# Corner products of 64x64 in place of block-diagonal 128x128 matrices in a chunked WKV recurrence

## The chip, the cores and the metric

One core of one Trainium2 chip runs the whole program, all in float32. The metric is the device time in microseconds of one execution. Engines are named as in the profile: PE is TensorE, PEld its weight loads, DVE is VectorE, ACT is ScalarE, POOL is GpSimd, SP issues most DMAs.

## The reference, cut to what matters

The program is a two-block network on 512 tokens with 256 context tokens. The first block mixes tokens by three methods, one of which is a recurrence over time with four heads of width 64, run in both directions:

```python
def wkv_scan(state0, r, kk, v, decay, b, k, reverse):
    def step(S, inp):
        r_t, kk_t, v_t, w_t, b_t, k_t = inp
        sa = jnp.einsum('bhij,bhj->bhi', S, kk_t)
        S = S * w_t[:, :, None, :] - sa[..., None] * b_t[:, :, None, :] + v_t[..., None] * k_t[:, :, None, :]
        return S, jnp.einsum('bhij,bhj->bhi', S, r_t)
    return lax.scan(step, state0, (r, kk, v, decay, b, k), reverse=reverse)
```

For each direction the 256 context tokens come first, then the 512 latent tokens start from the context's last state. Only latent outputs are used. Before and after the recurrence stand projections, two kinds of attention, a mixture of experts over 16384 rows, and a second block with its own attention and feed-forward layers.

## The kernel before, in words

The kernel doesn't step through tokens. It cuts time into 12 chunks of 64 tokens (0 to 3 context, 4 to 11 latent), and works each chunk in closed form: products of keys and values inside the chunk, the inverse of a 64x64 unit triangular matrix, and an update of the 64x64 state. There are eight such problems: two directions `d`, four heads. A head is `64*a` to `64*a+63` of the partitions with `a` 0 or 1, and a group `g`; the free index `s` is `2*d + g`, 0 to 3. So one PE step handles `s` = 0 to 3, each for two heads.

Before the change the two heads of an `s` stand in one 128x128 matrix as two diagonal blocks, with zeros off the diagonal; a matrix for all `s` is 128x512 and fills a PSUM bank. `Chunk.diagonal_blocks` (L1113) sets out `AB, BB, KB, VB, NT, M2`; `rwkv_zero_pool` (L1319) and L1521 zero their corners once.

`chunks` (L1748) takes chunks in pairs, and lets the two chunks of a pair take turns, step by step, on every engine; each engine runs its own in-order program and waits by semaphores. A chunk's part has three stretches.

- First products: `N`, `M1`, `M2` (L1420), masked by DVE (L1588, L1598, L1602), and the transposes `Bt`, `T0`, `Kt`, `Vt` (L1428), copied by ACT (L1552).
- The inverse: levels 1 to 4, each `X` = `NTo`' `Ta` (L1435, copied by ACT), `A` = `Tb`' `Xs` (L1435, added to `Ta` by DVE at L1613), and a transpose of `Ta` back to `Tb` (L1428, copied by DVE at L1617 or ACT). POOL masks `NTo` for the next level (L1632). Then `Y` and `inverse` close with two more products (L1621).
- The state, chunk by chunk: `RH` (L1673, L1674), its negative on DVE (L1713), `U` (L1681), copy (L1717), `sum` (L1688, L1689), add (L1721), four scalings (L1728). Latent chunks add the outputs (L1701 to L1703, L1740). The state update of a chunk needs that of the chunk before.

DVE, ACT and POOL prepare the inputs of chunk c+2 (`chunk_inputs_*`) between the levels of chunk c. PSUM banks: 0 to 2 for even chunks, 3 to 5 for odd ones, 6 and 7 for the state. After the recurrence come `first_half_pe` and the expert stage; eight loads of `w_out` wait for `state_filled` of chunk 10 (`out_weights_sp`).

Of the kernel before, what the change touches and what calls it, by code (L numbers as in the profile page):

```python
# [123 lines left out]
def constants():  # L124
# [966 lines left out]
MASKS = (("m_bk", 256), ("m_kk", 256), ("m_first", 128), ("m_last", 128), ("m_level", 256))  # L1091
# [4 lines left out]
class Chunk:  # L1096
# [3 lines left out]
    def __init__(self, A, B, ring, blocks_first, second, e1):  # L1100
        self.E1, self.KR = [B.take(2, 2, 65), e1.take(2, 2, 65)], [B.take(4, 2, 64), second.take(4, 2, 64)]
        if blocks_first:
            self.diagonal_blocks(A)
        self.at = A.at
        self.Bt, self.Kt, self.Vt, self.Ta, self.Tb, self.No, self.NTo = (A.take(4, P) for _ in range(7))
        self.M1R, self.M2R = A.take(4, 64), A.take(4, 64)
        self.E2 = second.take(2, 2, 64)
        self.Xs = A.take(4, P)
        if not blocks_first:
            self.diagonal_blocks(A)  # L1110
        self.AB = [self.AB, second.take(4, P)]
        self.ring = ring

    def diagonal_blocks(self, A):
        at = A.at
        self.AB, self.BB, self.KB, self.VB, self.NT, self.M2 = (A.take(4, P) for _ in range(6))
        self.blocks = A.t[:, at:A.at].rearrange("p (m s a n) -> p m s a n", m=6, s=4, a=2)
# [5 lines left out]
def rwkv_memory(k, rw, A):  # L1123
# [21 lines left out]
    rw.idb = k.ident[:, None, :].to_broadcast([P, 4, P])  # L1145
# [5 lines left out]
    rw.sets = [Chunk(slots, A, (0, 1, 2), False, free[0], Arena(k.SUMSQ, T)),  # L1151
               Chunk(A, A, (3, 4, 5), True, free[1], Arena(rw.Z[:, 8, :], TK))]
# [166 lines left out]
def rwkv_zero_pool(k, p):  # L1319

    S, rw = k.S, k.rw
    p.e.memset(rw.YT, 0.0).then_inc(*p.up(S.pool_scaled))
    p.wait_ge(S.ada_turned, 1)
    for j in (1, 0):
        for a in range(2):
            rows = slice(64 * a, 64 * a + 64)
            for m in range(6):
                p.in_order()
                p.e.memset(rw.sets[j].blocks[rows, m, :, 1 - a, :], 0.0).then_inc(
                    *(p.up(S.blocks_zeroed, j) if a and m == 5 else p.up(S.pool_scaled)))  # L1330
# [69 lines left out]
def by_direction(x):  # L1400

    return x.rearrange("p (d g n) -> p d g n", d=2, n=64)


def chunk_pe(k, p, c):
    S, rw = k.S, k.rw
    B, nk, x = rw.sets[c % 2], 2 if c >= 4 else 1, c // 2 % 2
    AB, KR = B.AB[x], B.KR[x]
    yield
    p.wait_ge(S.chunk_kept, (c, "inputs" if c >= 4 else "keys"))  # L1410
    p.wait_ge(S.chunk_prepared, (c, "inputs"))
    p.wait_ge(S.chunk_copied, (c, "inputs"))
    for step, (name, left, right, w) in enumerate((
            ("N", AB, lambda s: B.BB[:, s, :], P),
            ("M1", B.BB, lambda s: KR[:, s, 0:nk, :], 64 * nk),
            ("M2", B.KB, lambda s: KR[:, s, 0:nk, :], 64 * nk))):
        bank = chunk_bank(k, B, c, step)
        p.claim(chunk_place(B, c, step), S.chunk_kept, (c, name))
        for s in range(4):
            ins = p.e.matmul(bank[:, s * P:s * P + w], left[:, s, :], right(s), start=True, stop=True, skip_group_check=True)  # L1420
        ins.then_inc(*p.up(S.chunk_filled, (c, name)))
        yield

    def turned(step, name, src, signal):
        bank = chunk_bank(k, B, c, step)
        p.claim(chunk_place(B, c, step), signal, (c, name))
        for s in range(4):
            ins = p.e.transpose(bank[:, s * P:s * P + P], src[:, s, :], k.ident)  # L1428
        ins.then_inc(*p.up(S.chunk_filled, (c, name)))

    def products(step, name, left, right, signal):
        bank = chunk_bank(k, B, c, step)
        p.claim(chunk_place(B, c, step), signal, (c, name))
        for s in range(4):
            ins = p.e.matmul(bank[:, s * P:s * P + P], left[:, s, :], right[:, s, :], start=True, stop=True, skip_group_check=True)  # L1435
        ins.then_inc(*p.up(S.chunk_filled, (c, name)))

    turned(3, "Bt", B.BB, S.chunk_copied)
    yield
    p.wait_ge(S.chunk_kept, (c, "Ta"))  # L1440
    turned(4, "T0", B.Ta, S.chunk_copied)
    yield
    turned(5, "Kt", B.KB, S.chunk_copied)
    yield
    p.wait_ge(S.chunk_prepared, (c, "values"))
    turned(6, "Vt", B.VB, S.chunk_copied)
    yield
    for l in range(1, 5):
        p.wait_ge(S.chunk_prepared, (c, "NTo", l))
        products(4 + 3 * l, f"X{l}", B.NTo, B.Ta, S.chunk_copied)  # L1450
        yield
        p.wait_ge(S.chunk_copied, (c, f"X{l}"))
        p.wait_ge(S.chunk_copied if l % 2 else S.chunk_kept, (c, f"T{l - 1}"))
# [4 lines left out]
        yield  # L1458
    p.wait_ge(S.chunk_copied, (c, "T4"))
    products(19, "Y", B.No, B.Tb, S.chunk_copied)  # L1460
    yield
    p.wait_ge(S.chunk_copied, (c, "Y"))
    products(20, "inverse", B.Ta, B.Xs, S.chunk_kept)
    yield


def chunk_inputs_act(k, p, c):
# [13 lines left out]
    if c >= 4:  # L1481
        p.wait_ge(S.state_filled, (c - 4, "last"))
    p.wait_ge(S.chunk_kept, (c, "keys"))
    for a, h in enumerate(HEAD):
        p.e.activation(B.AB[x][h, :, h], B.KR[x][h, :, 0, :], ACT.Copy).then_inc(
            *(p.up(S.chunk_copied, (c, "inputs")) if a else p.up(S.scalar_step)))
    yield


def chunk_inputs_dve(k, p, c):  # L1490
# [23 lines left out]
def chunk_inputs_pool(k, p, c):  # L1514
    S, rw = k.S, k.rw
    B = rw.sets[c % 2]
    if c in (2, 3):
        p.wait_ge(S.bonus_product, 1)
        for a, h in enumerate(HEAD):
            p.in_order()  # L1520
            p.e.memset(B.AB[1].rearrange("p s (a n) -> p s a n", a=2)[h, :, 1 - a, :], 0.0).then_inc(*p.up(S.pool_scaled))  # L1521
# [3 lines left out]
    for h in HEAD:  # L1525
        p.in_order()
        p.e.tensor_tensor(B.KB[h, :, h].rearrange("p (d g) n -> p d g n", d=2), windows(rw.Kd, c, h), B.E2[h], ALU.mult).then_inc(
            *(p.up(S.chunk_prepared, (c, "inputs")) if h.start else p.up(S.pool_scaled)))
    yield
    if c >= 2:  # L1530
        p.wait_ge(S.chunk_filled, (c - 2, "Vt"))
    for d in range(2):
        for h in HEAD:
            p.in_order()
            p.e.tensor_copy(B.VB[h, SL[d], h], window(rw.V, c, d)[h]).then_inc(
                *(p.up(S.chunk_prepared, (c, "values")) if d and h.start else p.up(S.pool_scaled)))
# [3 lines left out]
def chunk_act(k, p, c):  # L1540
# [15 lines left out]
    for step, name, dst in ((3, "Bt", B.Bt), (4, "T0", B.Tb), (5, "Kt", B.Kt), (6, "Vt", B.Vt)):  # L1556
        copied(step, name, dst)
        yield
    for l in range(1, 5):
        copied(4 + 3 * l, f"X{l}", B.Xs)  # L1560
        yield
        if l in (1, 4):
            next(coming, None)
        yield
        if l % 2 == 0:
            copied(6 + 3 * l, f"T{l}", B.Tb)
        elif l == 1:
            next(coming, None)
        yield
    copied(19, "Y", B.Xs)  # L1570
    yield
    yield


def chunk_dve(k, p, c):
# [2641 lines left out]
```

## Time and profile before

| | |
|---|---|
| time, median of 3 runs | 3856.1 us (3851.97 to 3873.37) |
| the profiled execution's own time | 3852.21 us |
| its span | 3850.4 us |
| mean granted TensorE clock | 0.919 of 2.4 GHz |
| busy: PE, PEld, DVE, ACT, POOL | 85%, 63%, 55%, 20%, 36% |
| recurrence | 468.4 to 809.0 us of the span |

The profile gives one row for each of the two passes that a float32 product is run in, so a step of four products shows 8 matmul records and 8 weight loads; a transpose shows one. A form such as `128*128 128x64` reads: stationary operand 128 rows by 128 columns, moving operand 128 partitions by 64 columns. Records of the same kind that follow closely are merged in a timeline row: the second number is the time from the first's start to the last's end.

### The profile page before, as it was taken

What the parts mean: (1) busy time and instruction counts of PE and PEld (TensorE: products, weight loads), DVE (VectorE), ACT (ScalarE), POOL (GpSimd) and SP (SyncE); (2) the same over time, 40 slices, a digit from 0 to 9 for tenths busy, and PEclk for the clock granted to TensorE, in tenths of its full rate; (3) what the DMA queues carried; (4) which work ended last, traced back from release to release, by engine and by line L of the source; (5) the groups of instructions that cost most, each with busy time, mean ns of one, the idle gap of its engine ahead of it and who ended that gap; (6) DMA issues with size and microseconds to landing.
All of it is one profiled execution on the core that took longest, in us unless ns stands there. A gap on an engine that the chain in (4) does not pass through costs nothing. (4 is left out here: it accounts for less than half of the span.)

```text
span 3850.4 us, 39434 instructions
## 1 busy us (share of the span) xinstructions
PE 3280.3 (85%) x14438; PEld 2437.0 (63%) x14438; DVE 2121.7 (55%) x4234; ACT 764.9 (20%) x1791; POOL 1384.7 (36%) x1218
## 2 busy tenths in 40 slices
PE   8889888887677978647788888889897999999999
PEld 3566478775233535326567776667785778887787
DVE  2341345548889888867777668776653320133201
ACT  2231233222111111112420012320013210122100
POOL 0930022105677777754355546545500000000000
PEclk9998899998888989878689999889998999999999
DMA  6412100017999999987689999889941134431342
GB/s 206 129 66 82 31 1 1 13 44 275 363 368 373 373 374 384 393 308 276 208 288 376 394 377 371 302 282 392 394 145 34 60 125 150 147 99 61 126 152 100
DMA packets 424598, 831.77 MB, mean 216 GB/s; under 512 B 40467, under 2 KB 266830, under 8 KB 424398
## 3 DMA queue, kind: packets, MB, share of 16 engines
q0 software_dynamic: 147456, 536.94, 37.2%
q1 hardware_dynamic: 276950, 292.31, 23.3%
q8 instruction: 116, 1.90, 0.2%
q14 instruction: 76, 0.62, 0.0%
HBM read 826.98 MB, written 2.17 MB: 215 GB/s over the span
## 5 line engine op out<-in xcount | busy, mean ns | idle before, releaser
L2828 PE MATMUL banks<-arena 128*128 128x256 f32 (+1 forms) x4992 | 1142.4, 388 | 74.4 <-DMA arena<-in_l_w_up 30.4
L2828 PEld LDWEIGHTS banks<-arena 128*128 128x128 f32 (+1 forms) x4992 | 965.4, 195 | 236.8 <-issue 36.2
L2375 POOL DMA_INDIRECT arena<-in_peer_u,arena x512 | 577.6, 1128 | 456.4 <-DVE arena L2505 175.4
L2375 POOL DMA_INDIRECT arena<-in_peer_v,arena x512 | 590.5, 1153 | 400.5 <-DVE arena L2491 242.3
L2505 DVE CUSTOM_DVE_ANT_0 arena<-arena 128x1024 f32<-128x1024 f32 x512 | 628.1, 1227 | 104.4 <-DMA arena<-in_peer_u,arena 86.4
L2447 PE MATMUL banks<-arena 128*128 128x512 f32 x768 | 415.5, 685 | 188.5 <-ACT arena L2466 123.6
L2491 DVE SCALAR_TENSOR_TENSOR arena<-arena 128x1024 f32<-128x1024 f32 x316 | 406.3, 1286 | 29.4 <-DMA arena<-in_peer_v,arena 18.7
L2447 PEld LDWEIGHTS banks<-arena 128*128 128x128 f32 x768 | 159.7, 218 | 401.1 <-issue 246.4
L3737 PE MATMUL banks<-arena 128*128 128x256 f32 x1408 | 310.5, 378 | 0.0
L3786 DVE TENSOR_TENSOR arena<-banks,arena 128x512 f32<-128x512 f32 x44 | 30.5, 692 | 504.9 <-PE banks L2828 504.6
L3737 PEld LDWEIGHTS banks<-arena 128*128 128x128 f32 x1408 | 265.7, 189 | 38.3
L3758 ACT ACTIVATE arena<-banks 128x512 f32<-128x512 f32 x44 | 26.3, 597 | 684.7 <-PE banks L2828 679.7
L3279 DVE CUSTOM_DVE_ANT_0 arena<-banks,arena 128x256 f32<-128x256 f32 (+3 forms) x128 | 59.8, 467 | 138.6 <-PE banks L3161 131.4
L2140 PE MATMUL banks<-arena 128*128 128x512 f32 (+1 forms) x320 | 126.0, 542 | 9.4 <-DMA arena<-in_peer_q_w 5.9
L1632 POOL TENSOR_TENSOR arena<-arena 128x512 f32<-128x512 f32 x48 | 52.4, 1091 | 223.5 <-DVE arena L1598 119.1
L552 PE MATMUL banks<-arena 128*128 128x512 f32 (+1 forms) x336 | 132.1, 553 | 0.0
L812 PE MATMUL banks<-arena 128*128 128x512 f32 (+1 forms) x320 | 120.2, 525 | 5.7 <-ACT arena L455 3.6
L1552 ACT ACTIVATE arena<-banks 128x512 f32<-128x512 f32 x132 | 77.0, 597 | 223.9 <-PE banks L1428 173.2
L3231 ACT ACTIVATE arena<-arena 128x256 f32<-128x256 f32 (+3 forms) x128 | 69.3, 542 | 254.2 <-DVE arena L3279 185.0
L3202 PE MATMUL banks<-arena 128*128 128x64 f32 (+1 forms) x720 | 117.0, 296 | 1.5 <-ACT arena L3249 1.5
L3202 PEld LDWEIGHTS banks<-arena 128*128 128x128 f32 x720 | 111.8, 224 | 4.5 <-issue 2.6
L1435 PE MATMUL banks<-arena 128*128 128x128 f32 x960 | 114.5, 278 | 0.0
(341 smaller groups left out, 3883.7 us busy)
## 6 DMA issues: line engine op xcount, KB each, us to landing
arena<-in_l_w_gate SPq DMA_DIRECT2D x44, 1024.0 KB, 5.5
arena<-in_l_w_up SPq DMA_DIRECT2D x44, 1024.0 KB, 6.1
arena<-in_l_w_down SPq DMA_DIRECT2D x44, 1024.0 KB, 5.1
arena<-in_ada_w SPq DMA_DIRECT2D x24, 1024.0 KB, 7.6
arena<-in_l_w_qkv SPq DMA_DIRECT2D x24, 1024.0 KB, 6.4
arena<-in_w_in SPq DMA_DIRECT2D x33, 512.0 KB, 4.1
arena<-in_l_w_out SPq DMA_DIRECT2D x16, 1024.0 KB, 5.4
arena<-in_peer_q_w SPq DMA_DIRECT2D x10, 1024.0 KB, 12.4
```

The source lines that it names most:

```text
L552: ins = p.e.matmul(k.bank[b][0:m, 0:n], k.W[slot][:, c, 0:m], rhs(c), start=c == 0, stop=c == c_n - 1, skip_group_check=True)
L812: ins = p.e.matmul(k.bank[b][0:m, 0:n], k.W[slot][:, c, 0:m], rhs(c), start=c == 0, stop=c == c_n - 1, skip_group_check=True)
L1435: ins = p.e.matmul(bank[:, s * P:s * P + P], left[:, s, :], right[:, s, :], start=True, stop=True, skip_group_check=True)
L1552: p.e.activation(flat(dst), chunk_bank(k, B, c, step), ACT.Copy).then_inc(*p.up(S.chunk_copied, (c, name)))
L2140: ins = p.e.matmul(k.bank[4][:, cols], ws[:, c, P * j:P * j + P], k.HT[:, c, cols], start=c == 0, stop=c == DC - 1, skip_group_check=True)
L2375: p.e.indirect_dma_start(e.ring[slot], None, tables[table], bass.IndirectOffsetOnAxis(ap=e.IDX[h][:, t, j:j + 1], axis=0)).then_inc(*p.up( ...
L2447: ins = p.e.matmul(k.bank[b], e.diag[x % 4], e.ring[slot][:, half * T:half * T + T], start=h == 0 and j == 0, stop=h == HEADS - 1 and j == ...
L2491: p.e.scalar_tensor_tensor(out=e.ACC[t], in0=e.ring[slot], scalar=factor, in1=e.ACC[t], op0=ALU.mult, op1=ALU.add).then_inc(*p.up(S.rows_a ...
L2505: p.e.tensor_tensor_reduce(out=e.prod, in0=e.ring[slot], in1=e.H2[:, t, :], scale=1.0, scalar=0.0, op0=ALU.mult, op1=ALU.add, accum_out=e. ...
L2828: ins = p.e.matmul(out, left(c), right(c), start=c == 0, stop=c == c_n - 1, skip_group_check=True)
L3202: ins = p.e.matmul(k.bank[5][:, 0:x.w], a.PT[u % 2][:, j * P:j * P + P], values, start=j == 0, stop=j == len(x.values) - 1, skip_group_che ...
L3737: ins = p.e.matmul(k.bank[4 + o // 2][:, o % 2 * TH:o % 2 * TH + TH], w[:, r, P * o:P * o + P], a.hid[:, (i - 1) % 2, TH * r:TH * r + TH], ...
```

## The change

The two heads of an `s` now stand one above the other, 128x64 for each `s`, 128x256 for all, without zeros. Each product is of 64x64 corners: rows `HEAD[a]` as stationary and moving operand, output on partitions `HEAD[a]`. A step is eight matmuls in the order `CORNERS`, whose direction picks one of two neighbouring banks (a slot). PSUM becomes four slots of two banks, two for each chunk of a pair; the state uses slots 1 and 3 in turn. The inverse keeps both `Ta` and its transpose `Tb`: at each level `A` is added to `Ta` and `T` = `Xs`' `Tb` to `Tb`. There are five levels and no `Y`. The transposes `Bt`, `Kt`, `Vt` are products with an identity corner; `Vt` reads `rw.V` itself. `AB`, `VB`, the zeroing memsets and the copies into `AB` and `VB` go. In `state_pe`, `M2 Vt` and `Kt Vt` stand ahead of the waits. POOL also makes the first `Tb`. The loads, all other stages and the order of the stages are as before.

```diff
+STEPS = 20
+CORNERS = (0, 0), (1, 2), (0, 1), (1, 3), (1, 0), (0, 2), (1, 1), (0, 3)
+def slot_bank(slot, s):
+    return 2 * slot + s // 2
+def corner(k, slot, a, s, w=64):
+    return k.bank[slot_bank(slot, s)][HEAD[a], s % 2 * w:s % 2 * w + w]
+def slot_all(k, slot, w=64):
+    return k.PS[:, 1024 * slot:1024 * slot + 1024].rearrange("p (d x) -> p d x", d=2)[:, :, 0:2 * w].rearrange(
+        "p d (g n) -> p d g n", n=w)
+def chunk_slot(B, c, step):
+    return B.slots[(c // 2 * STEPS + step) % 2]
 def chunk_pe(k, p, c):
+    def products(step, name, left, right, signal, w=64):
+        slot = chunk_slot(B, c, step)
+        claim_slot(p, slot, signal, (c, name))
+        for a, s in CORNERS:
+            ins = p.e.matmul(corner(k, slot, a, s, w), left(a, s), right(a, s), start=True, stop=True, skip_group_check=True)
+        ins.then_inc(*p.up(S.chunk_filled, (c, name)))
...
-    turned(3, "Bt", B.BB, S.chunk_copied)
+    products(3, "Bt", of(B.BB), one, S.chunk_copied)
...
-    for l in range(1, 5):
+    for l in range(1, 6):
+        p.wait_ge(S.chunk_kept, (c, f"A{l - 1}"))
         p.wait_ge(S.chunk_prepared, (c, "NTo", l))
-        products(4 + 3 * l, f"X{l}", B.NTo, B.Ta, S.chunk_copied)
+        products(3 + 3 * l, f"X{l}", of(B.NTo), of(B.Ta), S.chunk_copied)
...
-        products(5 + 3 * l, f"A{l}", B.Tb, B.Xs, S.chunk_kept)
-        p.wait_ge(S.chunk_kept, (c, f"A{l}"))
-        turned(6 + 3 * l, f"T{l}", B.Ta, S.chunk_kept if l % 2 else S.chunk_copied)
-    products(19, "Y", B.No, B.Tb, S.chunk_copied)
-    products(20, "inverse", B.Ta, B.Xs, S.chunk_kept)
+        if l < 5:
+            products(4 + 3 * l, f"A{l}", of(B.Tb), of(B.Xs), S.chunk_kept)
+        products(5 + 3 * l if l < 5 else 19, f"T{l}", of(B.Xs), of(B.Tb), S.chunk_kept)
 def chunk_inputs_act(k, p, c):
-    for a, h in enumerate(HEAD):
-        p.e.activation(B.AB[x][h, :, h], B.KR[x][h, :, 0, :], ACT.Copy)
 def chunk_inputs_dve(k, p, c):
-    for h in HEAD:
-        p.e.tensor_tensor(B.BB[h, :, h]..., windows(rw.Bd, c, h), B.E2[h], ALU.mult)
+    p.e.tensor_tensor(by_direction(B.BB), windows(rw.Bd, c), B.E2, ALU.mult)
 def state_pe(k, p, c, between):
+    slot = state_slot(rw)          # 1 + 2 * (rw.turn % 2)
+    claim_slot(p, slot, S.state_kept, (c, "RH"))
+    p.wait_ge(S.chunk_kept, (c, "M2"))
+    p.wait_ge(S.chunk_copied, (c, "Vt"))
+    for a, s in CORNERS:
+        p.e.matmul(corner(k, slot, a, s), B.M2[HEAD[a], s, :], B.Vt[HEAD[a], s, :], start=s % 2 == 0, stop=False)
     p.wait_ge(S.state_ready, c - 1)
-    p.wait_ge(S.chunk_kept, (c, "inverse"))
+    for a, s in CORNERS:
+        ins = p.e.matmul(corner(k, slot, a, s), KR[HEAD[a], s, 0, :], S0[HEAD[a], s, :], start=False, stop=True)
...
```

## Rows read from the trace of the kernel before

**Rows 1.** the page's first part: busy time of each engine over the whole span
```profile
PE 3280.3 (85%) x14438; PEld 2437.0 (63%) x14438; DVE 2121.7 (55%) x4234; ACT 764.9 (20%) x1791; POOL 1384.7 (36%) x1218
```

**Rows 2.** stretches: busy us (records) of PE, PEld, DVE, ACT, POOL; clock; DMA; GB/s
```profile
471.84:809.03 337.19, 290.64 (x2296) 271.44 (x2296) 167.62 (x339) 91.51 (x172) 77.87 (x113) 0.96 0.03 10
...
511.52:526.75 15.23, 10.33 (x82) 9.38 (x81) 5.02 (x10) 0.00 (x0) 0.00 (x0) 1.00 0.00 1
```

**Rows 3.** timeline of TensorE: start, us, engine, line, records; first products of each pair
```profile
468.43 2.05 PE L1420 MATMUL banks<-arena 128*128 128x128 f32 x8 [5.69 <-ACT arena L1485]
...
526.75 5.47 PE L1420 MATMUL banks<-arena 128*128 128x128 f32 x48
...
578.01 5.52 PE L1420 MATMUL banks<-arena 128*128 128x128 f32 x48
...
637.48 5.58 PE L1420 MATMUL banks<-arena 128*128 128x128 f32 x48
...
695.18 5.58 PE L1420 MATMUL banks<-arena 128*128 128x128 f32 x48
...
751.53 5.58 PE L1420 MATMUL banks<-arena 128*128 128x128 f32 x48
...
809.03 3.62 PE L1777 MATMUL banks<-arena 128*128 128x256 f32 x8 [0.71 <-DVE arena L1740]
```

**Rows 4.** timeline, one level of the inverse in the latent pair at 578 us
```profile
591.09 3.80 PE L1435 MATMUL banks<-arena 128*128 128x128 f32 x32
...
592.18 0.60 ACT L1552 ACTIVATE arena<-banks 128x512 f32<-128x512 f32 x1 [0.30 <-PE banks L1435]
...
596.16 3.80 PE L1435 MATMUL banks<-arena 128*128 128x128 f32 x32
```

**Rows 5.** timeline, one chunk's state update near 792 us
```profile
791.48 1.16 PE L1681 MATMUL banks<-arena 128*128 128x128 f32 x8 [0.78 <-DVE arena L1713]
...
792.67 0.69 DVE L1717 COPY arena<-banks 128x512 f32<-128x512 f32 x1 [1.25 <-PE banks L1681]
...
796.31 0.87 DVE L1728 TENSOR_SCALAR arena<-arena 128x128 f32<-128x128 f32 x4
...
797.24 0.49 PE L1673 MATMUL banks<-arena 128*128 128x128 f32 x2 [1.76 <-DVE arena L1728]
```

**Rows 6.** groups by line and form, 500 to 800 us: busy, mean ns, idle before
```profile
L1632 POOL TENSOR_TENSOR arena<-arena 128x512 f32<-128x512 f32 x41 | 44.7, 1091 | 203.2 <-DVE arena L1598 113.9 <-PE banks L1435 54.2 <-DVE arena L1602 32.1
...
L1602 DVE TENSOR_TENSOR arena<-banks,arena 128x256 f32<-128x256 f32 x16 | 6.8, 425 | 0.5
...
L1475 ACT ACTIVATE arena<-arena 128x256 f32<-128x256 f32 x8 | 2.9, 412 | 0.1
```

**Rows 7.** timeline of TensorE, four bursts: two of attention, outputs, a prelude transpose
```profile
95.78 1.68 PE L812 MATMUL banks<-arena 128*128 128x256 f32 x7
...
99.49 1.15 PE L633 MATMUL banks<-arena 64*128 64x256 f32 x8 [0.51 <-ACTq L283]
...
628.84 0.39 PE L1703 MATMUL banks<-arena 128*128 128x64 f32 x2
...
54.10 0.41 PE L411 MATMUL banks<-arena 2*128 2x2 f32 x4
```

**Rows 8.** weight loads of two source lines: records, duration ns min/median/max, starts, forms
```profile
L1435 PEld LDWEIGHTS banks<-arena x960: 186/192/337, 486.0 to 788.3; 128*128 128x128 f32 x192
...
L3543 PEld LDWEIGHTS banks<-arena x64: 132/137/231, 1825.3 to 3013.7; 128*64 128x64 f32 x64
```

**Rows 9.** busy time by stretch, columns as in Rows 2: two neighbours in a pair, the recurrence's beginning
```profile
584.00:587.40 3.40, 1.72 (x12) 1.01 (x10) 3.21 (x10) 2.12 (x4) 2.18 (x2) 1.00 0.00 0
...
587.40:590.80 3.40, 3.17 (x14) 2.77 (x15) 1.23 (x4) 1.41 (x4) 0.00 (x0) 0.50 0.00 0
...
470.00:485.00 15.00, 13.64 (x65) 13.37 (x64) 7.86 (x16) 3.31 (x7) 3.83 (x7) 0.50 0.00 1
```

**Rows 10.** timeline, the loads after the recurrence
```profile
801.95 11.20 SPq L561 DMA_DIRECT2D arena<-in_w_out  x8
```

More of the change, by code:

```diff
@@ L1096, with __init__, inputs @@
 class Chunk:
-    def __init__(self, A, B, ring, blocks_first, second, e1):
+    def __init__(self, A, B, slots, blocks_first, second, e1, clear=0):
         self.E1, self.KR = [B.take(2, 2, 65), e1.take(2, 2, 65)], [B.take(4, 2, 64), second.take(4, 2, 64)]
         if blocks_first:
-            self.diagonal_blocks(A)
+            self.inputs(A)
         self.at = A.at
-        self.Bt, self.Kt, self.Vt, self.Ta, self.Tb, self.No, self.NTo = (A.take(4, P) for _ in range(7))
+        self.Bt, self.Kt, self.Vt, self.Ta, self.Tb, self.NTo, self.Xs = (A.take(4, 64) for _ in range(7))
         self.M1R, self.M2R = A.take(4, 64), A.take(4, 64)
         self.E2 = second.take(2, 2, 64)
-        self.Xs = A.take(4, P)
         if not blocks_first:
[L1110 to L1117, printed above, removed]
+            A.at = max(A.at, clear)
+            self.inputs(A)
+        self.slots = slots
+    def inputs(self, A):
+        self.BB, self.KB, self.NT, self.M2 = (A.take(4, 64) for _ in range(4))
 NCH = TK // 64
@@ L1319, in rwkv_zero_pool @@
 def rwkv_zero_pool(k, p):
[L1321 to L1330, printed above, removed]
+    p.e.memset(k.rw.YT, 0.0).then_inc(*p.up(k.S.outputs_zeroed, 0))
 def rwkv_begin(k, p):
@@ L1409, in chunk_pe, with one, values @@
+    def one(a, s):
+        return k.ident[HEAD[a], HEAD[a]]
+    def values(a, s):
+        at = first_token(c, s // 2)
+        return rw.V[HEAD[a], s % 2, at:at + 64]
     yield
     p.wait_ge(S.chunk_kept, (c, "inputs" if c >= 4 else "keys"))
+    products(0, "N", lambda a, s: KR[HEAD[a], s, 0, :], of(B.BB), S.chunk_kept)
+    yield
+    products(1, "M1", of(B.BB), lambda a, s: KR[HEAD[a], s, 0:nk, :], S.chunk_kept, 64 * nk)
+    yield
     p.wait_ge(S.chunk_prepared, (c, "inputs"))
-    p.wait_ge(S.chunk_copied, (c, "inputs"))
@@ L1413, in chunk_pe @@
[L1413 to L1436, printed above, removed]
@@ L1524, in chunk_inputs_pool @@
     p.wait_ge(S.decay_exp, (c, 2))
[L1525 to L1536, printed above, removed]
+    p.in_order()
+    p.e.tensor_tensor(by_direction(B.KB), windows(rw.Kd, c), B.E2, ALU.mult).then_inc(*p.up(S.chunk_prepared, (c, "inputs")))
     yield
@@ L1551, in copied @@
         p.wait_ge(S.chunk_filled, (c, name))
-        p.e.activation(flat(dst), chunk_bank(k, B, c, step), ACT.Copy).then_inc(*p.up(S.chunk_copied, (c, name)))
+        p.e.activation(by_direction(dst), slot_all(k, chunk_slot(B, c, step)), ACT.Copy).then_inc(*p.up(S.chunk_copied, (c, name)))
     for _ in range(3):
         yield
-    for step, name, dst in ((3, "Bt", B.Bt), (4, "T0", B.Tb), (5, "Kt", B.Kt), (6, "Vt", B.Vt)):
+    for step, name, dst in ((3, "Bt", B.Bt), (4, "Kt", B.Kt), (5, "Vt", B.Vt)):
         copied(step, name, dst)
         yield
-    for l in range(1, 5):
-        copied(4 + 3 * l, f"X{l}", B.Xs)
+    for l in range(1, 6):
+        copied(3 + 3 * l, f"X{l}", B.Xs)
         yield
-        if l in (1, 4):
+        if l in (1, 3):
             next(coming, None)
         yield
[L1565 to L1572, printed above, removed]
+        if l < 5:
+            yield
 def chunk_dve(k, p, c):
@@ L1601, in chunk_dve @@
         if latent:
-            p.e.tensor_tensor(rows.rearrange("p (d g) n -> p d g n", d=2), src[:, :, :, 64:P], m[:, :, :, 64:P],
-                              ALU.mult).then_inc(*p.up(S.chunk_kept, (c, name)))
+            p.e.tensor_tensor(by_direction(rows), src[:, :, :, 64:P], m[:, :, :, 64:P], ALU.mult).then_inc(
+                *p.up(S.chunk_kept, (c, name)))
         yield
-    for _ in range(4):
+    for _ in range(3):
         yield
-    for l in range(1, 5):
+    for l in range(1, 6):
@@ L1642, in chunk_pool, with state_slot @@
     p.wait_ge(S.chunk_kept, (c, "M1", "left") if latent else (c, "M1"))
-    off_diagonal(1)
-    for _ in range(6):
+    level(1, B.NTo, S.chunk_prepared, (c, "NTo", 1))
+    level(0, B.Tb, S.pool_scaled)
+    p.in_order()
+    p.e.tensor_tensor(B.Tb, B.Tb, rw.ones, ALU.add).then_inc(*p.up(S.chunk_prepared, (c, "Tb")))
+    for _ in range(5):
         yield
-    for l in range(1, 5):
-        if l < 4:
+    for l in range(1, 6):
+        if l < 5:
             p.wait_ge(S.chunk_filled, (c, f"X{l}"))
-            off_diagonal(l + 1)
-        if l >= 3:
+            level(l + 1, B.NTo, S.chunk_prepared, (c, "NTo", l + 1))
+        if l == 3:
             next(coming, None)
-        for _ in range(3):
+        yield
+        yield
+        if l < 5:
             yield
-    yield
-    yield
-def state_bank(rw):
+def state_slot(rw):
     rw.turn += 1
-    return 6 + rw.turn % 2
+    return 1 + 2 * (rw.turn % 2)
 def state_pe(k, p, c, between):
@@ L1666, in state_pe @@
     B, S0 = rw.sets[c % 2], rw.ST[c % 2]
[L1667 to L1674 removed]
+    KR = B.KR[c // 2 % 2]
@@ new lines, in state_pe @@
+    slot = state_slot(rw)
[3 more added lines that the diff above has]
+    for a, s in CORNERS:
+        p.e.matmul(corner(k, slot, a, s), B.M2[HEAD[a], s, :], B.Vt[HEAD[a], s, :], start=s % 2 == 0, stop=False,
+                   skip_group_check=True)
+    p.wait_ge(S.state_ready, c - 1)
+    for a, s in CORNERS:
+        ins = p.e.matmul(corner(k, slot, a, s), KR[HEAD[a], s, 0, :], S0[HEAD[a], s, :], start=False, stop=True,
+                         skip_group_check=True)
@@ L1675, in state_pe @@
     ins.then_inc(*p.up(S.state_filled, (c, "RH")))
     run(between)
-    b = state_bank(rw)
+    slot = state_slot(rw)
+    claim_slot(p, slot, S.state_kept, (c, "U"))
+    p.wait_ge(S.chunk_kept, (c, "T5"))
     p.wait_ge(S.state_kept, (c, "RH"))
-    p.claim(("bank", b), S.state_kept, (c, "U"))
-    for s in range(4):
-        ins = p.e.matmul(k.bank[b][:, s * P:s * P + P], B.Tb[:, s, :], rw.RH[:, s, :], start=True, stop=True, skip_group_check=True)
+    for a, s in CORNERS:
+        ins = p.e.matmul(corner(k, slot, a, s), B.Tb[HEAD[a], s, :], rw.RH[HEAD[a], s, :], start=True, stop=True,
+                         skip_group_check=True)
@@ L1682, in state_pe @@
     ins.then_inc(*p.up(S.state_filled, (c, "U")))
-    b = state_bank(rw)
-    p.wait_ge(S.state_kept, (c, "U"))
-    p.claim(("bank", b), S.state_kept, (c, "sum"))
-    for s in range(4):
-        o = k.bank[b][:, s * P:s * P + P]
-        p.e.matmul(o, B.Kt[:, s, :], B.Vt[:, s, :], start=True, stop=False, skip_group_check=True)
-        ins = p.e.matmul(o, B.Bt[:, s, :], rw.U[:, s, :], start=False, stop=True, skip_group_check=True)
+    slot = state_slot(rw)
+    claim_slot(p, slot, S.state_kept, (c, "sum"))
@@ L1690, in state_pe @@
+    for a, s in CORNERS:
+        p.e.matmul(corner(k, slot, a, s), B.Kt[HEAD[a], s, :], B.Vt[HEAD[a], s, :], start=s % 2 == 0, stop=False,
+                   skip_group_check=True)
+    p.wait_ge(S.state_kept, (c, "U"))
+    for a, s in CORNERS:
+        ins = p.e.matmul(corner(k, slot, a, s), B.Bt[HEAD[a], s, :], rw.U[HEAD[a], s, :], start=False, stop=True,
+                         skip_group_check=True)
     ins.then_inc(*p.up(S.state_filled, (c, "sum" if c >= 4 else "last")))
@@ L1696, in outputs_pe @@
     B, S0 = rw.sets[c % 2], rw.ST[c % 2]
-    b = state_bank(rw)
-    p.claim(("bank", b), S.outputs_added, c)
-    for s in range(4):
-        o = k.bank[b][:, s * 64:s * 64 + 64]
-        p.e.matmul(o, S0[:, s, :], B.KR[c // 2 % 2][:, s, 1, :], start=True, stop=False, skip_group_check=True)
-        p.e.matmul(o, B.Vt[:, s, :], B.M2R[:, s, :], start=False, stop=False, skip_group_check=True)
-        ins = p.e.matmul(o, rw.U[:, s, :], B.M1R[:, s, :], start=False, stop=True, skip_group_check=True)
+    KR = B.KR[c // 2 % 2]
+    slot = state_slot(rw)
+    claim_slot(p, slot, S.outputs_added, c)
+    for a, s in CORNERS:
+        p.e.matmul(corner(k, slot, a, s), S0[HEAD[a], s, :], KR[HEAD[a], s, 1, :], start=s % 2 == 0, stop=False,
+                   skip_group_check=True)
+    for a, s in CORNERS:
+        p.e.matmul(corner(k, slot, a, s), B.Vt[HEAD[a], s, :], B.M2R[HEAD[a], s, :], start=False, stop=False,
+                   skip_group_check=True)
+    for a, s in CORNERS:
+        ins = p.e.matmul(corner(k, slot, a, s), rw.U[HEAD[a], s, :], B.M1R[HEAD[a], s, :], start=False, stop=True,
+                         skip_group_check=True)
     ins.then_inc(*p.up(S.state_filled, (c, "last")))
@@ L1733, in outputs_dve @@
     S, rw = k.S, k.rw
-    b = state_bank(rw)
+    slot = state_slot(rw)
     p.wait_ge(S.state_filled, (c, "last"))
```

135 lines of the change are left out of this document (54 added, 81 removed).

## The prediction

> **What bounds the kernel now.** I read the page first: PE is busy 85% of the span, far above any other engine [rows 1]. Then the stretches: in the recurrence, 471.84 to 809.03 us, PE is busy 290.6 of 337.2 us, DVE 167.6, ACT and POOL under 92 each, and DMA 3% [rows 2]. So this stage depends on PE and on the turns that PE takes with DVE and ACT. The timeline of PE cuts it into six pairs of chunks [rows 3]: from `N` to `N` the pairs take 58.3, 51.3, 59.5, 57.7, 56.4 and 57.5 us, 340.6 together. A latent pair is some 38 us of first products and inverse, and 20 of state and outputs.
>
> Inside a level PE hardly stops: 32 product records take 3.80 us, that is (3.80 - 0.28)/31 = 0.114 a record, and the level returns after 5.07 us (591.09 to 596.16) [rows 4]. The state update is the other kind: PE gives eight records (1.16 us), DVE copies 512 columns (0.69 us), and so three times over, then four scalings (0.87 us) [rows 5]; a context pair's two updates take 15.2 us, of which PE is busy 10.3 [rows 2]. So shorter PE steps and half as wide copies both count, and both are on the path.
>
> **The new step.** Before, a step is 4 matrices x 2 passes = 8 records (a transpose 4). After, it is 8 corners x 2 = 16. The whole question is what a corner's record costs.
> - Its own price. Records are 0.112 us apart with 128 stationary and 128 moving columns, and still so with 64 moving ((0.39 - 0.28) us between two of L1703 [rows 7]): the weight load of 128 columns holds them. A load of 64 columns takes 137 ns against 192 [rows 8], 55 ns less. So a record with 64 of each should take 0.112 - 0.055 = 0.057 us; I take 0.058 (estimate).
> - Overlap. The attention's scores use rows 0 to 63 and 64 to 127 in turn, as the corners will. Eight such records of 256 columns take 1.15 us; seven of full height take 1.68 us, 0.217 apart, so eight in line would be 1.90 [rows 7]. 1.15 is four slots of 0.215 and a tail: two records run at once. Corners differ in columns of the array too, which no row here shows; nothing speaks against it.
> - `CORNERS` takes the halves in turn except once in the middle and once between steps, so a step is 8 slots at best and 10 at worst. I take 9: 9 x 0.058 = 0.52 us, against 8 x 0.112 = 0.90 for a product step and half for transposes. `M1` and `M2` of latent chunks move 128 columns: 9 x 0.112 = 1.0 us.
> - Bounds for a step: 0.46 (8 slots) below; above, 0.93 (16 slots of 0.058, no overlap) and 1.79 (16 x 0.112, neither gain).
>
> **The copies.** A DVE operation on 128x256 from banks takes 0.43 us (L1602) for 0.69, ACT on 128x256 0.41 (L1475; from SBUF, so a bound at best) for 0.60 [rows 4 to 6]. POOL's mask at 128x512 takes 1.09; half as wide I take 0.58. From a step's last slot to its end are 0.21 us (1.16 - 8 x 0.112 = 0.26, less 0.05 for the shorter record), then 0.04 to the copy and 0.06 back to PE [rows 5]. So a dependent hop by DVE is 0.52 + 0.21 + 0.04 + 0.43 + 0.06 = 1.26 us.
>
> **Part by part, a latent pair.**
> - First products: `N` 2 x 0.52, `M1` and `M2` 4 x 1.0, `Bt`, `Kt`, `Vt` 6 x 0.52: 8.2 us. Before: 13.1 (578.01 to 591.09). The transposes get dearer (0.52 for 0.45), but `T0` goes, and so do PE's waits for DVE's half-height masks. POOL has three operations for each chunk here, 1.8 us, from about 3 us on; `NTo` of both is ready at 5.5, so it is hidden. If POOL took as long as before (1.09) the second `Tb` would come at about 9.6, still ahead of its `A`.
> - A level: `X` of both, `A` waits 0.52 + 0.21 + 0.04 + 0.41 + 0.06 = 1.24 from the first `X`, then `A`, `A`, `T`, `T`: 1.24 + 2.08 = 3.32 us for 5.07. The next `X` needs only the first `A` in `Ta` (1.24 + 1.26 = 2.5), so DVE's four adds (1.9 us) are covered. The fifth level has no `A`: 2.28. Together 4 x 3.32 + 2.28 = 15.6. Before: 4 x 5.07, and `Y` and `inverse` with two hops, some 25.
> - The join. The state's first slot is the one of the last `T`, so `M2 Vt` waits for that add: 0.74 + 0.52 = 1.3 us, partly new.
> - State: three hops and four scalings at half width (0.66 + 0.06, estimate from 0.87): 4.5 us. Before it is 5.76 from `U` to the next `RH` [rows 5], and `RH` itself 16 x 0.112 + 0.26 + 0.79: 8.6. `M2 Vt` and `Kt Vt` are issued while PE waits for DVE. The second chunk with both chunks' outputs: 0.52 + 1.56 (outputs cover the negative) + 1.26 + 0.52 + 1.56 = 5.4.
> - Sum: 8.2 + 15.6 + 1.3 + 4.5 + 5.4 = 35.0 us. Four latent pairs: 140 for 231.0, -91 us.
>
> The second context pair: 12 steps 6.2, then 15.6 + 1.3 + 2 x 4.5 = 32.1 for 51.3: -19. The first runs at 0.5 of the clock, 1.2 GHz, for at least 15 us (PE sat idle 5.7 us before it) [rows 3, 9]; there PE steps double, +8: 40.1 for 58.3, -18. The first `N` comes about 2 us earlier, since the copies into `AB` and one of two half-height products go. Sum -91 - 19 - 18 - 2 = -130.
>
> Against it: DVE's input products (levels 2 and 3) fill it up there, one adding some 0.5 to 1 us to a pair, and in-order waits that I can't place; I allow 10 us. And the clock: in 584.0 to 587.4 PE was busy half the time, and the next 3.4 us ran at 0.5 [rows 9]. The pair that holds this took 59.5 us against 57.5 [rows 3]. The shorter state steps leave gaps of that kind; I allow 7 us. Net -113.
>
> Behind the recurrence nothing gives it back: the `w_out` loads are issued after chunk 10's state (801.95 [rows 10]) and PE wants the first of them after the head means (809.03 + 3.4 [rows 3]), 10.5 us later; after the change about 8, by the sum above. That leaves cover for the first two; if it were gone, each late load costs some 1.4 us (11.2 / 8), at most 3. POOL, whose memsets go, is busy 36% [rows 1] and waits before the recurrence. The stages after shift as a block.
>
> The profiled execution took 3852.2 us; 3852.2 - 113 = 3739. The median is 3.9 above it, so I forecast 3743.
>
> **A rule against it.** In the prelude, four weight load and matmul pairs of 2 columns take 0.41 us, (0.41 - 0.22)/3 = 0.063 us apart [rows 7], though the array has little to do. The Trainium skill, "TensorE: Matmul & The Clock Gate", section "Wait - 56ns, not 53.3ns?", says that where the hardware decoder is off the sequencer spends about 62 ns on each MATMUL, and that this binds once the array's work is shorter. If each pass is one such, a step is 16 x 0.062 = 0.99 us by that page, an estimate. This row agrees with it; the attention's burst decides nothing, as its eight records take longer than eight such intervals.
>
> **The rivals.**
> - No gain from pairs (corners of different columns don't overlap, or issue holds a record at about 0.06). A step is 0.93 us; a level then is PE-bound at 6 steps, 5.6 us; the latent pair 14.6 + 26.0 + 1.7 + 5.7 + 9.1 = 57.1 for 57.7, a context pair 50.3. All told -7 us, and at 0.063 a record +10: 3849 to 3866. For it: the prelude's row. Against: the attention's. Chance 0.11.
> - The clock stays at half for most of the stage because PE has more gaps. A record is 0.112 at that clock: a step 1.0, latent pair 61.5 (+3.8), context 54: about +12, 3868; for half of the stage, about 3805. For it: [rows 9]. Against: 511.5 to 526.8, with PE busy 68%, ran at 1.00 throughout [rows 2]. Chance 0.04.
> - Slower: a record costs 0.112 us whatever its size, as if each load and matmul had a fixed price. There are 16 for 8, so with no overlap a step is 1.79 us, a level 10.7, a latent pair 99 and the whole some 4095; with overlap in pairs, a step of 1.0, it is +12. The change loses from a step of about 0.95 us on. For it: halving the moving columns brought nothing in the outputs [rows 7]. Against: the narrower load is shorter in its own record [rows 8]. Chance 0.07 for a loss over 0.5%.
> - My forecast and its neighbours, 8 to 10 slots and more or fewer cold stretches: 0.78.
>
> **Numbers.** At 8 slots a pair is about 5 us shorter, 3715; at 10 slots with 20 us more of waits, about 3790. The likeliest case alone is 3712 to 3795. To leave out no more than 2 in 10 the range goes into the partly cold case: 3715 to 3830. Half a percent is 19 us, about what a measurement can tell. Faster: 0.78 and part of the clock case, 0.80; same: most of the first rival, 0.12; slower: 0.08.
>
> **What would show it.** The pairs' starts 33 to 38 us apart; 16 records of `X` in about 0.75 us to the last end, with starts in twos a few ns apart; levels of 3.3 us; DVE adds of 0.43 us at 128x256; state updates of 4.5 us; the stage over by about 700 us. Starts evenly 0.06 apart would show the first rival, 0.11 the slower one. I am wrong if a product step takes over 0.9 us, or if DVE or ACT, not PE, sets the level.

## The result and the profile after

The changed kernel takes 3721.5 us (median of 4 runs, 3716.3 to 3735.0) against 3862.3 (4 runs): a ratio of 0.9644, 95% interval 0.9622 to 0.9665. Measured twice more on other occasions it gave 0.9646 (0.9626 to 0.9665) and 0.9624 (0.9599 to 0.9648). The forecast was 3743, in a range of 3715 to 3830, so it was right; how much of that was luck follows below.

The profiled executions, 3852.2 and 3721.8 us, differ by 130.4. The recurrence accounts for more than all of it: from the first `N` to the head means it took 340.6 us and takes 205.4. It began 3.9 us later, and what follows took 0.9 us more (3041.4 and 3042.3). So -135.2 + 3.9 + 0.9 = -130.4. In these two executions the stages behind took nothing of the gain away. From profile to profile they vary by up to 25 us (below), so a smaller effect of theirs is not shown.

Busy times by stretch, columns as in rows 2: the whole recurrence, the two updates of a context pair, and two latent pairs from `N` to `N`.

```profile
472.35:677.71 205.36, 179.23 (x5184) 169.62 (x5184) 118.47 (x321) 42.97 (x116) 61.20 (x95) 0.98 0.05 13
...
496.30:504.30 8.00, 5.79 (x161) 5.14 (x162) 2.87 (x9) 0.00 (x0) 0.00 (x0) 1.00 0.01 2
...
536.05:572.15 36.10, 31.74 (x902) 30.31 (x900) 21.68 (x61) 7.36 (x20) 10.32 (x16) 0.95 0.01 3
...
572.15:607.20 35.05, 30.54 (x902) 28.97 (x900) 21.37 (x59) 7.37 (x20) 10.33 (x16) 1.00 0.01 4
```

PE has 5184 records in the stage, where it had 2304, and is busy 179 us for 293. The whole stage before, from its first `N`:

```profile
468.43:809.03 340.60, 292.69 (x2304) 273.22 (x2304) 170.74 (x344) 92.84 (x176) 80.75 (x119) 0.96 0.03 9
```

From `N` to `N` the pairs take 32.0, 31.8, 36.1, 35.1, 36.2 and 34.3 us [rows 3 for before]. The first of the two latent pairs holds a stretch at half the clock, and is 1.05 us longer.

Where the time of a step went is seen in the timeline of TensorE, outputs of a latent chunk. Each line has 16 records; the next line starts 0.46 to 0.47 us after it.

```profile
567.48 0.63 PE L1677 MATMUL banks<-arena 64*64 64x64 f32 x16
...
567.94 0.63 PE L1680 MATMUL banks<-arena 64*64 64x64 f32 x16
```

That is 8 slots of 0.058 us with two records in each, which start 5 to 6 ns apart (576.612 and 576.617 us). Where PE doesn't wait, 128 records take 3.74 us (576.61 to 580.35), 0.467 for 16. Groups by line and form say the same of the operands: a copy on ACT went from 597 to 383 ns, an add on DVE from 692 to 425, POOL's mask from 1091 to 645 [rows 6].

```profile
L1598 POOL TENSOR_TENSOR arena<-arena 128x256 f32<-128x256 f32 x72 | 46.4, 645 | 126.9 <-DVE arena L1572 88.4 <-PE banks L1423 33.3
...
L1558 DVE TENSOR_TENSOR arena<-banks,arena 128x256 f32<-128x256 f32 x108 | 45.9, 425 | 47.1 <-PE banks L1423 39.0
...
L1529 ACT ACTIVATE arena<-banks 128x256 f32<-128x256 f32 x96 | 36.8, 383 | 150.6 <-PE banks L1423 145.3
```

One thing is late now. The timeline from level 1 to level 4 of the pair at 572 us, DVE and PE:

```profile
583.19 1.68 DVE L1491 TENSOR_TENSOR arena<-arena 128x256 f32<-128x256 f32 x2
...
585.33 2.01 DVE L1558 TENSOR_TENSOR arena<-banks,arena 128x256 f32<-128x256 f32 x4 [0.46 <-PE banks L1423]
...
585.80 3.32 PE L1423 MATMUL banks<-arena 64*64 64x64 f32 x96 [0.16 <-DVE arena L1558]
...
590.55 2.01 DVE L1558 TENSOR_TENSOR arena<-banks,arena 128x256 f32<-128x256 f32 x4
...
591.03 5.42 PE L1423 MATMUL banks<-arena 64*64 64x64 f32 x160 [1.91 <-DVE arena L1558]
```

At 583.19 DVE makes `BB` for both next chunks, and PE comes a little late (0.16). In the next level it makes the keys, eight products ahead of the adds, and PE stands still for 1.91 us. That level takes 5.23 us and the one with `BB` 3.36, where the first takes 3.03.

### The profile page after: what moved, and what is told of

It reads as the page before. It is cut to its first block and busy times, and to the rows that moved or that the text cites. A ratio compares the mean times of both kernels' runs of the same rounds, so it can differ in the third digit from the quotient of the medians.

```text
span 3720.0 us, 45189 instructions
## 1 busy us (share of the span) xinstructions
PE 3169.8 (85%) x17318; PEld 2333.8 (63%) x17318; DVE 2070.2 (56%) x4210; ACT 714.6 (19%) x1731; POOL 1356.9 (36%) x1166
## 5 line engine op out<-in xcount | busy, mean ns | idle before, releaser
L2428 PEld LDWEIGHTS banks<-arena 128*128 128x128 f32 x768 | 159.2, 218 | 405.6 <-issue 251.3
L3718 PEld LDWEIGHTS banks<-arena 128*128 128x128 f32 x1408 | 265.8, 189 | 38.3
L3739 ACT ACTIVATE arena<-banks 128x512 f32<-128x512 f32 x44 | 26.3, 598 | 683.5 <-PE banks L2809 678.4
L1423 PE MATMUL banks<-arena 64*64 64x64 f32 (+1 forms) x3840 | 134.0, 228 | 14.2 <-DVE arena L1558 8.5
L1423 PEld LDWEIGHTS banks<-arena 64*64 64x64 f32 x3840 | 128.3, 139 | 20.2 <-DVE arena L1558 9.4
L3183 PEld LDWEIGHTS banks<-arena 128*128 128x128 f32 x720 | 112.0, 224 | 4.5 <-issue 2.6
L2121 PEld LDWEIGHTS banks<-arena 128*128 128x128 f32 x320 | 65.1, 205 | 68.3 <-issue 59.1
```

Source lines behind the costliest of these rows:

```text
L1423: ins = p.e.matmul(corner(k, slot, a, s, w), left(a, s), right(a, s), start=True, stop=True, skip_group_check=True)
L2121: ins = p.e.matmul(k.bank[4][:, cols], ws[:, c, P * j:P * j + P], k.HT[:, c, cols], start=c == 0, stop=c == DC - 1, skip_group_check=True)
L2428: ins = p.e.matmul(k.bank[b], e.diag[x % 4], e.ring[slot][:, half * T:half * T + T], start=h == 0 and j == 0, stop=h == HEADS - 1 and j == ...
L3183: ins = p.e.matmul(k.bank[5][:, 0:x.w], a.PT[u % 2][:, j * P:j * P + P], values, start=j == 0, stop=j == len(x.values) - 1, skip_group_che ...
L3718: ins = p.e.matmul(k.bank[4 + o // 2][:, o % 2 * TH:o % 2 * TH + TH], w[:, r, P * o:P * o + P], a.hid[:, (i - 1) % 2, TH * r:TH * r + TH], ...
```

## The experiments

**The changed kernel again**, as a yardstick for the next three.

> The changed kernel itself, unaltered, as the yardstick on the chip of the next three. From its first measurement (3721.5 us, 0.9644 of before) both theories expect 0.961 to 0.967 of before, and the recurrence at 205 us of the span.

It gave 3733.7 us, 0.9646 (0.9626 to 0.9665); the recurrence took 205.1 us. The recurrence's time from the trace repeats within 0.5 us, while what follows it took between 3041 and 3067 us over all profiles, though no edit touched it. So below, "recurrence" is the sharper number for edits inside it.

**No turns.**

```diff
-CORNERS = (0, 0), (1, 2), (0, 1), (1, 3), (1, 0), (0, 2), (1, 1), (0, 3)
+CORNERS = (0, 0), (0, 2), (0, 1), (0, 3), (1, 0), (1, 2), (1, 1), (1, 3)
```

> Only the order of the eight corners is changed: the four of partitions 0 to 63 first, then the four of 64 to 127; directions still take turns, so neighbours write to different banks. Theory (the step is short because records of the two halves run at once, 0.058 us a slot of two, 8 slots): neighbours now share rows, a step becomes some 16 slots of 0.058 = 0.93 us, and with 12 + 28 + 10 to 16 steps a pair the time returns to nearly that of before: +125 to +140 us over the changed kernel, 3840 to 3870. Rival (the step is short because records are small, and the array or its queue orders them itself): starts stay about 0.47 us for 16, the time within 5 us of the changed kernel.

It gave 3769.5 us, 0.9731 (0.9708 to 0.9755), recurrence 244.4: +36 us and +39 us, some 4 of which are the clock (24 us at half speed in the recurrence for 10). Both expectations fail. 2.3 us of a level hold 64 starts (69 records with those in flight), 0.575 us a step: 10 slots, neither 8 nor 16.

```profile
599.50:601.80 2.30, 2.30 (x69) 1.00 0.03 7
```

Why it isn't 16 stands in the timeline of TensorE of this kernel, at the seam of two lines. In program order all 16 records of L1641 come before those of L1645:

```profile
496.79 0.50 PE L1641 MATMUL banks<-arena 64*64 64x64 f32 x8
...
497.07 0.27 PE L1645 MATMUL banks<-arena 64*64 64x64 f32 x1
...
497.12 0.22 PE L1641 MATMUL banks<-arena 64*64 64x64 f32 x1
...
497.18 0.22 PE L1645 MATMUL banks<-arena 64*64 64x64 f32 x1
...
497.18 0.22 PE L1641 MATMUL banks<-arena 64*64 64x64 f32 x1
...
497.24 0.22 PE L1641 MATMUL banks<-arena 64*64 64x64 f32 x1
```

L1645 starts on partitions 0 to 63 while L1641 still works on 64 to 127. Three records of L1641 start after the first of L1645. The two halves advance separately, and overlap runs across the seams of steps as well.

**One bank.**

```diff
-CORNERS = (0, 0), (1, 2), (0, 1), (1, 3), (1, 0), (0, 2), (1, 1), (0, 3)
+CORNERS = (0, 0), (1, 0), (0, 2), (1, 2), (0, 1), (1, 1), (0, 3), (1, 3)
```

> Only the order is changed: the halves take turns strictly, and both of a neighbouring pair write to the same bank (other partitions of it). Theory A (rows alone decide): the step stays at 8 slots, 0.47 us, within 5 us of the changed kernel. Theory B (two records can't write one bank at a time, so the pair goes one behind the other): 16 slots, 0.93 us a step, +120 us or more, as without turns.

3732.9 us, 0.9648 (0.9626 to 0.9670), recurrence 204.8. Theory A: it costs nothing that two concurrent records write to other partitions of one bank. The care of `CORNERS` for banks was not needed for speed. The Trainium skill, "TensorEngine Tiling (Array Packing)", section "Restrictions and Gotchas", says that different row tiles can't access the same PSUM bank at once. For these corners, whose columns differ as well, the run shows no cost of such a rule.

**Runs of eight**, to see how far a half runs ahead.

```diff
+RUNS = ((0, 0), (0, 2), (0, 1), (0, 3), (1, 0), (1, 2), (1, 1), (1, 3)), (
+       (1, 0), (1, 2), (1, 1), (1, 3), (0, 0), (0, 2), (0, 1), (0, 3))
-        for a, s in CORNERS:
+        for a, s in RUNS[c % 2]:
```

> The corners of the first products and of the inverse go in runs: an even chunk does its four of partitions 0 to 63 and then the other four, an odd one the other way round, so PE gets eight matmuls (16 records) of one half on end. The state's steps keep their turns. In the run without turns (four on end) a step took 0.575 us and records of a later line started ahead of the last of an earlier one. Theory (each half has a stream of its own that runs ahead, as far as what is already issued allows): with twice as long runs less overlaps, a step of 0.65 to 0.93 us and 50 to 110 us over the changed kernel. Rival (the streams run ahead without a limit): the step stays near 0.58 us and the time within 10 us of the run without turns.

3806.8 us, 0.9828 (0.9802 to 0.9855), recurrence 281.7, +77 us. Part of that is the clock, which stood at half from 465 to 523 us: the first pair takes 63.6 us and the second, at the full clock, 40.0, so some 24 of the 77 us. In a stretch without waits, at the full clock, 160 records take 7.54 us, 0.754 a step or 13 slots:

```profile
594.06:601.60 7.54, 7.54 (x160) 1.00 0.02 4
```

The rival (0.58 us) is out and the theory's 0.65 to 0.93 holds. The two runs agree on how far a half gets ahead: with runs of four a step has two changes of half and 16 - 10 = 6 slots are saved, with runs of eight one change and 16 - 13 = 3, so three slots at each change. Without any change a step would then take 16 slots; that is carried on from 8, 10 and 13, not measured. A slot is 0.058 us in all of them. So the change had two gains of PE: a narrow record takes 0.058 us in place of 0.112, which alone would only pay for there being twice as many, and overlap halves what is left. The new order of the inverse, `T` beside `A` with no transpose after the add, was not run by itself. By an estimate from rows it is the smaller part: PE's steps in a level were 4 x 0.90 + 2 x 0.45 = 4.5 of 5.07 us and are 2.80 of 3.04, so the waits that it could shorten fell from 0.57 to 0.24 us.

**State copies twice.**

```diff
+    p.e.tensor_scalar(by_direction(rw.RH), slot_all(k, slot), -1.0, None, ALU.mult).then_inc(*p.up(S.vector_step))
+    p.in_order()
...
+    p.e.tensor_copy(by_direction(rw.U), slot_all(k, slot)).then_inc(*p.up(S.vector_step))
+    p.in_order()
```

> DVE makes the negative of RH and the copy of U twice over, from the same bank to the same place, 24 more operations of 0.42 us. Theory (each hop of the state stands bare on the path, so a copy half as wide gives its whole 0.27 us): each costs 0.42 to 0.48, save the negative of the second chunk of the four latent pairs, which the outputs cover: +8 to +11 us over the changed kernel. Rival (PE's steps cover it): within 3 us.

3739.1 us, 0.9651 (0.9622 to 0.9679), recurrence 214.26 for 205.15: +9.1, with one more stretch of half clock (3.4 us) than the yardstick. The program's own time can't tell 9 us here (+5 against the yardstick of the other occasion), the trace can. A context pair's updates went from 8.00 to 9.84 us at the full clock, 0.46 for each of four operations; a latent pair's from 10.15 to 11.40, three at 0.42. So these copies stand on the path with their whole length.

**X copies twice.**

```diff
+        if name[0] == "X":
+            p.e.activation(by_direction(dst), slot_all(k, chunk_slot(B, c, step)), ACT.Copy).then_inc(*p.up(S.scalar_step))
+            p.in_order()
```

> ACT copies X twice, from the same slot to the same place, 60 more operations of 0.38 us. Theory (in a level PE waits 0.24 us for the first copy, and nothing else is spare there): the first A comes 0.42 later and the second one more 0.3, so a level takes 0.4 to 0.8 us longer in 30 levels less what DVE's own delay in level 3 covers: +10 to +22 us. Rival (level is bound by DVE's adds): within 4 us.

3746.2 us, 0.9677 (0.9652 to 0.9702), recurrence 218.9, +13.8: inside the expectation, 0.46 us for each of 30 levels. This recurrence has one stretch of half clock where the yardstick has three; at 1.05 us each [the pairs above] the copies cost some 15.9 us, 0.53 a level. In the levels without DVE's input products it is 0.64. The copies of `X` are on the path too, in part behind the `X` of the other chunk and the wait of level 3.

**Keys early.**

```diff
 def chunk_act:
+    run(coming)                      # both exponentials at the chunk's start
...
-        if l in (1, 3):
-            next(coming, None)
...
 def chunk_dve:
-    for _ in range(3):
+    for i in range(3):
+        if i == 1 and c + 2 < NCH:
+            chunk_keys_dve(k, p, c + 2)
         yield
     for l in range(1, 6):
-        if l in (2, 3):
-            next(coming, None)
+        if l == 2 and c + 2 < NCH:
+            chunk_products_dve(k, p, c + 2)
```

> DVE's products for KR of chunk c+2 are moved from level 3 of chunk c to the time of Bt, Kt, Vt, where DVE waits for 3.7 us; ACT makes both exponentials at the start of a chunk. Theory (in level 3 PE waits 2.1 us for DVE, since four products for each chunk stand ahead of the adds): that wait goes in five pairs, -8 to -11 us, recurrence at 195 us. Rival (something else would be late there, POOL's mask or ACT's copy): the level still takes 5 us and the time stays within 3 us.

3717.4 us, 0.9615 (0.9588 to 0.9643), recurrence 192.4: -12.7, more than expected. In the timeline of this kernel PE goes without a listed wait from the first products to the state:

```profile
559.84 19.38 PE L1423 MATMUL banks<-arena 64*64 64x128 f32 x582
...
562.80 0.85 DVE L1502 TENSOR_TENSOR arena<-arena 128x128 f32<-128x128 f32 x2
...
568.85 1.33 DVE L1491 TENSOR_TENSOR arena<-arena 128x256 f32<-128x256 f32 x2
...
579.82 0.68 PE L1646 MATMUL banks<-arena 64*64 64x64 f32 x16 [0.59 <-DVE arena L1561]
```

The keys now stand at 562.80, where DVE had nothing to do, and the first four levels take 3.03 to 3.13 us. The pair takes 32.5 us for 35.05. The edit moves ACT's exponentials together with the keys that need them; neither was moved alone. The rest of the gain is two stretches of half clock that don't occur: this recurrence has one, at its start, where the changed kernel has three.

**And the product split, the scalings made one.**

```diff
-        if l == 2 and c + 2 < NCH:
+        if l == 2 + c % 2 and c + 2 < NCH:
...
-    for s in range(4):
-        p.e.tensor_scalar(S1[:, s, :], rw.sum[:, s, :], e1, None, ALU.mult)
+    e1 = both_directions(B.E1[c // 2 % 2][:, 0, :, 64:65], 2 * 65 - 64)
+    p.e.tensor_tensor(by_direction(S1), by_direction(rw.sum), e1.to_broadcast([P, 2, 2, 64]), ALU.mult)
```

> The keys are early, as in the run before (it measured 0.9615 of before, against 0.9646 of the changed kernel); besides, the product BB of an odd chunk is moved a level later than that of the even one, and the four scalings of a state update are one product of 128x256 with the decay broadcast. Theory (PE still waits 0.4 us at level 2, and 0.92 for the four scalings of 0.74 us, where one product takes 0.42): -0.3 us x 12 and -0.3 us x 5, some -5 us more: 0.958 to 0.962 of before. Rival (broadcast in a product costs as much as the four, or DVE's order makes another wait): as the run before, 0.9615 or over.

3713.5 us, 0.9602 (0.9573 to 0.9630), recurrence 190.3: -2.1 against the run before, for some -5 expected. Two timelines show the scaling, first the changed kernel, then this one: four operations of 0.74 us in all and a wait of 0.92, then one of 0.42 and a wait of 0.60.

```profile
566.16 0.74 DVE L1709 TENSOR_SCALAR arena<-arena 128x64 f32<-128x64 f32 x4
...
566.96 0.68 PE L1645 MATMUL banks<-arena 64*64 64x64 f32 x16 [0.92 <-DVE arena L1709]
```

```profile
559.07 0.42 DVE L1711 TENSOR_TENSOR arena<-arena 128x256 f32<-128x256 f32 x1
...
559.55 0.62 PE L1650 MATMUL banks<-arena 64*64 64x64 f32 x14 [0.60 <-DVE arena L1711]
```

A scaling on the path saves 0.31 us. A latent pair has one, not two, since PE needs the second chunk's state only after the next pair's inverse; it went from 32.5 to 32.1 us. The second context pair fell by 0.62: 0.31 in its state update, and 0.31 in its first products, where PE waits for DVE's masks and DVE is done with the scaling before them (that of the former pair's last chunk) sooner. The split gave the remaining 0.09 us of a latent pair, since moving the keys had already cut the wait at level 2.

**Both once more, beside each other.**

> The changed kernel unaltered, beside the next one on the same chip: 0.9645 of before, recurrence 205 us of the span.

> The version with early keys, the split and the single scaling, unaltered, for a second measurement beside the changed kernel. Its recurrence took 190.3 us of the span against 205.1. Theory (what the recurrence saves is saved by the program): 15 us less than the changed kernel, 0.9605. Rival (the stages behind, whose own time moved by up to 24 us from profile to profile, take some of it back, by other phases of clock and DMA): less than 8 us apart.

The changed kernel 3721.4 us, 0.9624 (0.9599 to 0.9648), recurrence 204.9; the version 3709.1 us, 0.9601 (0.9575 to 0.9627), recurrence 190.0. By medians the program is 12.4 us faster, between the theory's 15 and the rival's 8. The ratios' intervals overlap, so of the program's time that is likely, not shown; the 14.9 us in the recurrence are.

## Why the prediction was right, point by point

- **The bound.** PE and its turns with DVE and ACT set the stage, and still do. With the keys early a level is six steps of 0.467 and waits of 0.24 in all for the first copy, 3.04 us; 3.3 was predicted.
- **The step.** A record was taken as 0.058 us, from a shorter weight load of another line; it is 0.058. I took 9 slots; it is 8. The seam in the middle of `CORNERS` costs nothing: strictly alternating halves (one bank) took the same time. `M1` and `M2` take 0.88 us for 1.0. For 8 slots the text has a pair "about 5 us shorter"; some 57 steps by 0.058 are 3.3 us at most.
- **The copies.** 0.43 us on DVE was 0.425; ACT's 0.41 was 0.383, POOL's 0.58 was 0.645. Counted as in the prediction, from `RH` on, the first chunk's update took 4.45 us (4.5), the second with all outputs 5.2 (5.4). The second of a context pair took 3.0 for 4.5: the sum charged the pair for its last hop and its scalings, for which the next pair's first products don't wait.
- **The latent pair.** 35.0 predicted, 35.05 measured, and that close by luck. The pair from 572.15 has 7.3 us of first products (8.2), 16.9 of inverse (15.6), 1.2 for the join (1.3) and 9.7 of state and outputs (9.9). The shorter step should have brought the inverse down too, but DVE's input products ahead of the adds cost 2.2 us in level 3 and 0.3 in level 2, for which I allowed 0.5 to 1 us a pair, and not within the 35.0. Without them the pair takes 32.5. I had this queue in the text and its time in rows (eight products ahead of the adds), and did not add it up for the level in which it stands.
- **The first pair.** I carried over the 15 us and more at half clock from before, +8 us. After the change it was 3.4 us, and the pair took 32.0 us for 40.1. That is the largest term that was off. In the other runs that stretch was 3.4 us eight times, 6.8 without turns, and 58 with runs of eight. What ends it isn't settled.
- **The allowances.** 10 us for waits went to the keys (five pairs at 2.1), 7 us for the clock were not needed: after the first stretch the recurrence has two at half clock, before it had four. The price of one was misread, too: the pair of 59.5 us before holds two such stretches (587.4 and 621.5), the one from 695.18 none and took 56.4, so one costs 1.1 to 1.6 us there and not 2. The pairs summed to -128 before allowances and measured -135, the first pair making the difference; all told net -113 was forecast and -130 measured in the profiled executions.
- **Start and end.** `N` came 3.9 us later, not 2 earlier; in the other profiles of the changed kernel it came at 464.7 and 468.8, so this is spread of the stages before. The loads of `w_out` weren't late: PE takes the first at 679.54, 5.8 us after its issue at 673.76 (8 in the prediction), without a wait.
- **The rivals.** Issue at 0.06 a record: wrong, two weight loads and two matmuls go in 0.058 us, 15 ns each, for as long as a stretch lasts; so the prelude's 0.063 us a pair [rows 7] isn't what every matmul costs in issue. The Trainium skill ("TensorE: Matmul & The Clock Gate", section "Wait - 56ns, not 53.3ns?") gives 62 ns for each MATMUL where the hardware decoder is off. Matmuls here come every 29 ns (0.467/16), so that price isn't paid; no run shows how the decoder is set. The clock: granted at 0.98 on the mean of the stage. A fixed price a record: wrong. But the first rival's time would have been the outcome if the halves didn't overlap: 16 slots of 0.058, 0.93 us, are about what the step took before (0.90). The largest run length tried, eight, still had 13.

## What to carry to other kernels

Two 64-row problems side by side in zeros cost as much as full matrices; as corners on their own partitions a product step takes about half (0.467 us for 0.90) and a transpose the same (0.467 for 0.45), and that only because the two halves of the array run at once, so give them work in turn and check that starts come in twos. When an engine's steps shrink, add up for each step what the other in-order engines hold ahead of the result it waits for: there the next microseconds are. And judge such an edit by the stage in the trace, as the rest of the program moved more than the edit.

## What the runs showed of the hardware

- Records of the two row halves are not held to one order: a later instruction of one half started before three records of an earlier one of the other half (497.07 against 497.12, 497.18 and 497.24 us).
- With runs of four or eight matmuls of one half, three slots of a step are shared at each change of half: 10 and 13 slots for 16 records.
- A 64x64 float32 record takes one slot of 0.058 us at the full clock, also when PE issues four instructions a slot.
- Concurrent records of these corners, on other partitions and columns, write one bank at no cost (recurrence 204.8 us against 205.1).
- At its start the recurrence ran at half the clock for 3.4 us in nine runs, 6.8 without turns, 17 us before the change and 58 us with runs of eight, though PE was busy 95 to 100% of those 58 us:

```profile
465.00:500.00 35.00, 35.00 (x420) 34.84 (x418) 7.92 (x21) 5.51 (x16) 8.07 (x13) 0.50 0.01 2
...
523.00:560.00 37.00, 33.95 (x741) 33.29 (x737) 17.12 (x48) 7.37 (x20) 10.44 (x16) 1.00 0.01 2
```

The clock stayed at half through 35 us in which PE's records leave no gap. Of the orders tried, the one with the least overlap has the longest slow stretch, but the kernel before, with none, has 17 us. What decides was not found.
